# Rotary halves exchanged by ScalarE copies instead of permutation matmuls

## The chip, the cores and the metric

The kernel runs on one core of a Trainium2 chip. The metric is the device time of one execution in microseconds, the median of several runs. The engines are named as in the profile: PE is TensorE (its weight loads are PEld), DVE is VectorE, ACT is ScalarE, POOL is GpSimd, SP is SyncE, whose queue streams the weights. A matmul with fp32 operands is one instruction in the program; the trace shows it as two.

## What is computed

A chain of transformer blocks over 512 tokens of width 1024, all in fp32: a sparse-attention mixer, a state-space mixer, then an "even" mixer, a feed-forward block, an "odd" mixer and a second feed-forward block. The change is in the even mixer, which runs stick-breaking attention (8 heads of 64) and retention (4 heads of 128) on one projection:

```
p = hn @ w_in
sb_q, sb_k, sb_v, r_q, r_k, r_v, r_g = jnp.split(p, cuts, axis=-1)
...
qb = rope(to_heads(r_q, RET_HEADS), pos)
kb = rope(to_heads(r_k, RET_HEADS), pos)
...
def rope(x, pos):
    ...
    x1, x2 = xf[..., :half], xf[..., half:]
    return jnp.concatenate([x1 * cos - x2 * sin, x1 * sin + x2 * cos], axis=-1)
```

With features on the partitions, rope is x * cos + swapped(x) * sin, where swapped(x) has the upper 64 features, negated, in the lower 64 partitions and the lower 64 in the upper.

## The kernel before

Everything is one hand-written program with an instruction list for each engine; nothing schedules them but their order and the semaphores. Activations lie with 128 features on the partitions and the 512 tokens on the free axis. Each product with a weight matrix is done in three fp32r matmuls per 128x128 block: high part of the weights by high part of the input, high by low, low by high. A tile of weights (128 output features, 8 blocks, 512 KB) lands in a ring of four, DVE rounds it to its high part `whi` (L172), POOL subtracts to get `wlo` (L164, L152), and PE multiplies (24 matmuls a tile).

The even mixer has 28 such tiles, seven for each i = 0 to 3: q, k, v of a pair of stick-breaking heads and rq, rk, rv, rg of one retention head. PE runs the first four tiles by themselves (L339 to L341), and the others in quarters of six matmuls (L596 to L598, `product_beside`) between the small matmuls of the attention. `pe_stick` and then `pe_retention` run for each i; a tuple of numbers says how many quarters come between their steps. In `pe_retention` three quarters (18 matmuls) stand between the swap matmuls and the scores; for i = 3, where no tiles are left, three blocks of the next stage's product (9 matmuls, L989 to L991, `pe_even_out_beside`) stand there instead.

The steps around the change, for each i:

- ACT: take rv out of PSUM (L822), then rg with a Silu (L743), which has a table load ahead of it, and a second table load behind it (L794) back to the set with Exp and Ln; then take the stick-breaking output from bank 7 (`eo_h`, L825), once PE has done its last stick matmul (L728, semaphore `e_o`).
- DVE: rqt and rkt by the cosine (L916, into `et`), the rounding of a weight tile, then `eo_l` (L919), the low part of the stick output, which waits for L825 (semaphore `e_oh`); then, in `dve_retention`, the products of the swapped halves with the sine (L1032, from banks 2 and 3 into `el`), and the sums (L1035) that make the rotated query `rqs` and key `rks`; then the scores by the decay (L1039).
- PE: the stick output (L728), the swap matmuls (L950) of rqt and rkt with the 128x128 permutation `swap` into banks 2 and 3, the quarters, the four score matmuls (L955), which wait for both sums of L1035 (semaphore `r_qkv`), more quarters, the weighted sum (L960), and so on to `eo_l` of the retention head (L1054).

At the start of the stage `act_even` issues three loads on ACT's queue, `etab` (tables), `egain` and `swap`, and waits for all three (L759) before it takes the first tile with L736 (Square) and L737 (Copy); L737 frees the accumulator for PE's third tile. PE waits for the same three loads once, at L647.

Of the kernel before, what the change touches and what calls it, by code (L numbers as in the profile page):

```python
# [14 lines left out]
P = 128  # L15
# [32 lines left out]
def build(nc, A, out, names=tuple(s[0] for s in STAGES)):  # L48
# [5 lines left out]
    with ExitStack() as ctx:  # L54
# [32 lines left out]
        def at(name, shape, dt=F32, offset=None):  # L87

            size = int(np.prod(shape[1:])) * 4
            offset = used[0] if offset is None else offset  # L90
            used[0] = offset + (size + 63) // 64 * 64
            assert used[0] <= nc.sbuf_usable_end, (name, used[0])
            return nc.alloc_sbuf_tensor_at(name, shape, dt, offset=offset)
# [416 lines left out]
        decay = etab[:, 3 * P + 2 * S:3 * P + 6 * S].rearrange("p (r s) -> p r s", r=4)  # L510
        e64eps = etab[:, 3 * P + 6 * S:3 * P + 6 * S + 1]
        egain = at("egain", [P, 3])
        swap = at("swap", [P, P])
        eq, ek, ev = (at(name, [P, S]) for name in ("eq", "ek", "ev"))
        rqt, rkt, rvt, rgt = (at(name, [P, S]) for name in ("rqt", "rkt", "rvt", "rgt"))
        qs = at("qs", [P, S])
# [113 lines left out]
        def even_taken(engine, name, i):  # L630

            r = even_tile(name, i)
            engine.wait_ge(acc_free[r % 2], freed(O0["even_in"] + r))
# [10 lines left out]
        def pe_head_squares(pe, i):  # L644

            if i == 0:
                pe.wait_ge(e_loaded, 48)  # L647
            for j in range(2):
                pe.wait_ge(e_sqr, 2 * i + j + 1)
                nc.tensor.matmul(bank[2 + j][:], bdiag, et[:, 2 + j, :], start=True, stop=True).then_inc(e_ms, 1)  # L650
# [104 lines left out]
        def act_even(act):  # L755
            act.dma_start(etab[:], A["even_tables"]).then_inc(e_loaded, 16)
            act.dma_start(egain[:], A["even_gains"]).then_inc(e_loaded, 16)
            act.dma_start(swap[:], A["swap"]).then_inc(e_loaded, 16)
            act.wait_ge(e_loaded, 48)  # L759
            act_head_tile(act, "q", 0, eq)  # L760
            act_head_tile(act, "k", 0, ek)
            act_even_tile(act, "v", 0, sq[:, 0, :])
            act.preload_act_table_set(LOG_EXP)
            act_head_rstd(act, 0)
            act_even_tile(act, "rq", 0, rqt[:])
            for i in range(4):
                act_stick(act, i)
                act_retention(act, i)

        def act_stick(act, i):  # L770

            def soft(u):
                hd, jb, w = unit(u)
                act.wait_ge(e_z, 8 * i + u + 1)
                if u >= 2:
                    act.wait_ge(e_t, 8 * i + u - 1)
                if u == 1 and i:
                    act.wait_ge(r_m, i)
                nc.scalar.activation(ea[:, hd, 0:w], bank[2 + u % 3][:, 0:w], ACT.Abs).then_inc(e_abs, 1)
                act.wait_ge(e_abs, 2 * (8 * i + u) + 1)  # L780
                nc.scalar.activation(ea[:, hd, 0:w], ea[:, hd, 0:w], ACT.Exp, scale=-1.0).then_inc(e_abs, 1)
                act.wait_ge(e_abs, 2 * (8 * i + u) + 2)
                nc.scalar.activation(el[:, hd, 0:w], ea[:, hd, 0:w], ACT.Ln, bias=ones[:, 0:1]).then_inc(e_l, 1)

            def weight(u):
                hd, jb, w = unit(u)
                act.wait_ge(e_t2, 8 * i + u + 1)
                nc.scalar.activation(packed(ew, hd, jb), et[:, u % 4, 0:w], ACT.Exp).then_inc(e_w0, 1)

            def tile(place):  # L790
                name = dict(zip("ACEF" if i else "BDF", EVEN[3:] if i else EVEN[4:])).get(place)
                if name == "rg":
                    act_even_tile(act, "rg", i, rgt[:], ACT.Silu)
                    act.preload_act_table_set(LOG_EXP)  # L794
                elif name is not None:
                    act_even_tile(act, name, i, {"rq": rqt[:], "rk": rkt[:], "rv": sq[:, 1, :]}[name])

            soft(0)
            soft(1)
            tile("A")  # L800
            act.wait_ge(tv_turned, TV0["even_in"] + 2 * i + 1)
            nc.scalar.activation(ev[:], bank[7][:], ACT.Copy).then_inc(tv_taken, 1)
            soft(2)
            soft(3)
            tile("B")
            weight(0)
            weight(1)
            soft(4)
            soft(5)
            tile("C")  # L810
            weight(2)
            weight(3)
            tile("D")
            soft(6)
            soft(7)
            weight(4)
            weight(5)
            tile("E")
            weight(6)
            weight(7)  # L820
            act.wait_ge(tv_turned, TV0["even_in"] + 2 * i + 2)
            nc.scalar.activation(rvt[:], bank[4][:], ACT.Copy).then_inc(tv_taken, 1)  # L822
            tile("F")
            act.wait_ge(e_o, i + 1)
            nc.scalar.activation(eo_h[:, i, :], bank[7][:], ACT.Copy).then_inc(e_oh, 1)  # L825

# [117 lines left out]
        def pe_retention(pe, i, beside):  # L944

            between = iter((3, 4, 2, 3) if i < 3 else (3, 3, 1, 7))
            pe.wait_ge(e_t, 8 * i + 8)
            for j in range(2):
                even_taken(pe, ("rq", "rk")[j], i)
                nc.tensor.matmul(bank[2 + j][:], swap[:], (rqt, rkt)[j][:], start=True, stop=True).then_inc(r_rot, 1)  # L950
            beside(next(between))
            pe.wait_ge(tv_taken, TV0["even_in"] + 2 * i + 2)
            pe.wait_ge(r_qkv, 2 * i + 2)
            for jb in RORDER:
                nc.tensor.matmul(retention_scores(jb), rks[:, jb * P:(jb + 1) * P], rqs[:, jb * P:S],  # L955
                                 start=True, stop=True).then_inc(r_s, 1)
            beside(next(between))
            for jb in range(4):
                pe.wait_ge(r_w, 4 * i + RORDER.index(jb) + 1)
                mm = nc.tensor.matmul(bank[6][:, jb * P:S], rvt[:, jb * P:(jb + 1) * P], packed(ew, 0, jb),  # L960
                                      start=jb == 0, stop=jb == 3)
            mm.then_inc(r_o, 1)
            beside(next(between))
            pe.wait_ge(r_sq, i + 1)
            nc.tensor.matmul(bank[5][:], ones, ea[:, 0, :], start=True, stop=True).then_inc(r_ms, 1)
            if i < 3:
                pe_head_squares(pe, i + 1)
            beside(next(between))
# [59 lines left out]
        def dve_retention(dve, i):  # L1028

            for j in range(2):  # L1030
                dve.wait_ge(r_rot, 2 * i + j + 1)
                nc.vector.tensor_tensor(el[:, j, :], bank[2 + j][:], sin_t, ALU.mult).then_inc(r_part, 1)  # L1032
            for j in range(2):
                dve.wait_ge(r_part, 4 * i + 3 + j)
                nc.vector.tensor_tensor((rqs, rks)[j][:], et[:, j, :], el[:, j, :], ALU.add).then_inc(r_qkv, 1)  # L1035
            dve.wait_ge(e_o, i + 1)
            for jb in RORDER:
                dve.wait_ge(r_s, 4 * i + {0: 1, 2: 2}.get(jb, 4))
                nc.vector.tensor_tensor(packed(ew, 0, jb), retention_scores(jb), decay[:, i, 0:S - jb * P],  # L1039
                                        ALU.mult).then_inc(r_w, 1)  # L1040
            if i < 3:
                dve_even_split(dve, "q", i + 1)
                dve_even_split(dve, "k", i + 1)
            dve.wait_ge(r_r, i + 1)
            nc.vector.scalar_tensor_tensor(et[:, 0, :], bank[6][:], egain[:, 2:3], ea[:, 1, :],
                                           ALU.mult, ALU.mult).then_inc(r_m, 1)
            dve.wait_ge(r_m, i + 1)
            even_taken(dve, "rg", i)
            nc.vector.tensor_tensor(rmix[:], et[:, 0, :], rgt[:], ALU.mult).then_inc(r_mix, 1)
            if i < 3:  # L1050
                dve_head_scaled(dve, i + 1)
                dve_even_split(dve, "v", i + 1)
            dve.wait_ge(r_hi, i + 1)
            nc.vector.tensor_tensor(eo_l[:, 4 + i, :], rmix[:], eo_h[:, 4 + i, :].bitcast(F32),  # L1054
                                    ALU.subtract).then_inc(r_lo, 1)
# [1941 lines left out]
        dec.append(np.where(d >= 0, np.exp(lg * np.maximum(d, 0)) * P ** -0.5, 0.0))  # L2997
    return np.concatenate([bd, later, before, cc, sc, *dec, np.full((P, 4), 64e-6)], 1).astype(np.float32)

def host_swap():  # L3000

    w = np.zeros((P, P), np.float32)
    for m in range(64):
        w[m + 64, m] = -1
        w[m, m + 64] = 1
    return w

def by_state(v):

    n = v.ndim  # L3010
# [8 lines left out]
def host_arrays(I, names):  # L3019
# [8 lines left out]
        cv[:, l, 3] = cols(I['ffn_conv_b_2'][l])  # L3028
    a['conv'] = cv
    a['even_tables'] = host_even_tables()  # L3030
    a['swap'] = host_swap()
    q, k = I['sb_q_gain_2'][0], I['sb_k_gain_2'][0]
    a['even_gains'] = np.stack([np.concatenate([q, q]), np.concatenate([k, k]), I['ret_out_gain_2'][0]], 1)
    p, c = np.arange(P)[:, None], np.arange(S)[None, :] % P
# [46 lines left out]
```

## Time and profile before

| | |
|---|---|
| median of 3 runs | 2058.25 us (2058.07 to 2058.46) |
| the profiled execution | 2057.75 us, its span 2055.9 us |
| PE busy | 1969.3 us (96%) |
| DVE busy | 1113.0 us (54%) |
| POOL busy | 793.9 us (39%) |
| ACT busy | 607.0 us (30%) |

The span goes from the first to the last instruction of the trace; the profiled execution is 1.85 us longer than its span. The even mixer lies between 760 and 1060 us of it. In the timelines a row gives start, duration, engine, line of the kernel, operation, output and input, and in brackets how long the engine was idle before it and who released it. The starts of PE's matmuls are what counts: their ends are modelled, so that a matmul of 0.39 us may be followed by the next after 0.23.

### The profile page before, as it was taken

The numbers are of one execution on the slowest core, as the hardware profiler recorded it, in microseconds if no ns is written. First come the engines' busy times: TensorE is split into PE (matmuls) and PEld (weight loads), VectorE is DVE, ScalarE is ACT, GpSimd is POOL, SyncE is SP. The second block draws the span as 40 slices with busy tenths as digits, with TensorE's granted clock in tenths as the row PEclk, the third lists the DMA queues.
The fourth block names the chain that finished last, engine by engine and source line by source line (L and its number), as shares of the span: only waits on it lengthen the run. The fifth ranks groups of instructions, "written<-read, shape, count | busy, mean of one in ns | idle before, by whom it ended". The sixth has DMA issues, their size and how long they took to land.

```text
span 2055.9 us, 26747 instructions
## 1 busy us (share of the span) xinstructions
PE 1969.3 (96%) x9876; PEld 1531.0 (74%) x9876; DVE 1113.0 (54%) x2063; ACT 607.0 (30%) x1164; POOL 793.9 (39%) x430
## 2 busy tenths in 40 slices
PE   8999999978999969999999999999999999999999
PEld 5867776757778746766678888887578878888887
DVE  5679998886774444445565454312533355454311
ACT  3136656125651135444422111100422222111100
POOL 3532222336663433222234444444133234444443
PEclk9999999989999989999999999999999999999999
DMA  5611111212212222111122232333122122222232
GB/s 182 178 62 42 33 41 42 82 51 66 71 49 95 92 66 83 62 62 51 52 82 94 92 102 92 102 102 104 62 72 69 66 84 93 99 95 95 100 123 72
DMA packets 55300, 167.66 MB, mean 82 GB/s; under 512 B 8080, under 2 KB 16144, under 8 KB 54816
## 3 DMA queue, kind: packets, MB, share of 16 engines
q1 hardware_dynamic: 47904, 155.22, 22.4%
q10 hardware_dynamic: 7296, 11.09, 2.0%
q8 instruction: 65, 1.06, 0.2%
q14 instruction: 35, 0.29, 0.0%
HBM read 157.90 MB, written 2.10 MB: 78 GB/s over the span
## 4 chain that ended last, share of the span: by engine, by line
issue 38%; PE 34%; POOL 15%; DVE 8%; SPq 4%; DMA 0%; POOLq 0%; ACT 0%; DVEq 0%; ACTq 0%
POOL wlo L164 14%; PE bank L181 7%; PE bank L182 7%; PE bank L183 7%; SPq L146 4%; DVE prob L1674 2%; DVE ssb L1661 2%; PE bank L2655 1%; PE bank L2656 1%; PE bank L2657 1%; PE bank L1296 1%; PE bank L1321 1%; PE bank L1239 1%; PE bank L1237 1%; DVE probt L1682 1%
## 5 line engine op out<-in xcount | busy, mean ns | idle before, releaser
L164 POOL TENSOR_TENSOR wlo<-raw,whi 128x1024 fp32r<-128x1024 f32 x248 | 597.7, 2410 | 957.4 <-DVE whi L172 957.4
L172 DVE CAST whi<-raw 128x1024 fp32r<-128x1024 f32 x288 | 203.8, 708 | 418.3 <-PE bank L183 227.6
L181 PE MATMUL bank<-xh,whi 128*128 128x512 f32 x704 | 276.3, 392 | 8.8 <-POOL wlo L164 8.8
L182 PE MATMUL bank<-xl,whi 128*128 128x512 f32 x704 | 275.3, 391 | 0.0
L183 PE MATMUL bank<-xh,wlo 128*128 128x512 f32 x704 | 275.2, 391 | 0.0
L596 PE MATMUL bank<-xh,whi 128*128 128x512 f32 x424 | 177.1, 418 | 1.5 <-POOL wlo L164 1.5
L598 PE MATMUL bank<-xh,wlo 128*128 128x512 f32 x424 | 166.1, 392 | 0.0
L597 PE MATMUL bank<-xl,whi 128*128 128x512 f32 x424 | 165.3, 390 | 0.0
L181 PEld LDWEIGHTS bank<-xh,whi 128*128 128x128 f32 x704 | 133.0, 189 | 38.1 <-POOL wlo L164 10.1
L183 PEld LDWEIGHTS bank<-xh,wlo 128*128 128x128 f32 x704 | 133.1, 189 | 28.1
L182 PEld LDWEIGHTS bank<-xl,whi 128*128 128x128 f32 x704 | 133.2, 189 | 27.3
L183 PE MATMUL bank<-ghi,wlo 128*128 128x512 f32 x352 | 139.1, 395 | 0.0
L181 PE MATMUL bank<-ghi,whi 128*128 128x512 f32 x352 | 139.0, 395 | 0.0
L182 PE MATMUL bank<-glo,whi 128*128 128x512 f32 x352 | 139.0, 395 | 0.0
L1722 POOL TENSOR_TENSOR wlo<-raw,whi 128x1024 fp32r<-128x1024 f32 x22 | 52.0, 2364 | 151.7 <-DVE whi L172 151.7
L596 PEld LDWEIGHTS bank<-xh,whi 128*128 128x128 f32 x424 | 79.7, 188 | 27.5 <-issue 13.2
L598 PEld LDWEIGHTS bank<-xh,wlo 128*128 128x128 f32 x424 | 79.6, 188 | 17.7
L597 PEld LDWEIGHTS bank<-xl,whi 128*128 128x128 f32 x424 | 79.9, 188 | 16.4 <-issue 2.2
L1674 DVE TENSOR_SCALAR prob<-prob,gsig,stat 128x128 f32<-128x128 f32 (+3 forms) x128 | 89.3, 739 | 2.3
L478 DVE TENSOR_TENSOR upad<-bank,rstd 128x512 f32<-128x512 f32 x44 | 30.5, 693 | 102.7 <-PE bank L183 87.4
L225 ACT ACTIVATE bank<-h 128x512 f32<-128x512 f32 x42 | 25.2, 601 | 205.8 <-DVE h L402 199.3
L491 DVE TENSOR_TENSOR bank<-bank,rstd 128x512 f32<-128x512 f32 x44 | 30.8, 699 | 99.4 <-PE bank L183 94.3
(387 smaller groups left out, 3900.7 us busy)
## 6 DMA issues: line engine op xcount, KB each, us to landing
raw<-in_weights_dram SPq DMA_DIRECT2D x288, 512.0 KB, 3.2
h<-in_x_dram SPq DMA_DIRECT2D x2, 1024.0 KB, 7.4
sz<-su SPq DMA_DIRECT2D x128, 16.0 KB, 1.8
out_dram<-h ACTq DMA_DIRECT2D x4, 512.0 KB, 2.6
etab<-in_even_tables_dram ACTq DMA_DIRECT2D x1, 1730.0 KB, 6.5
x_kh<-kvc_h ACTq DMA_DIRECT2D x2, 256.0 KB, 5.0
x_kl<-kvc_l ACTq DMA_DIRECT2D x2, 256.0 KB, 7.0
x_vh<-kvc_h ACTq DMA_DIRECT2D x2, 256.0 KB, 5.0
```

What stands on the lines that cost most here:

```text
L146: sp.dma_start(sz[32 * r:32 * r + 32, j, q * P:(q + 1) * P], su[32 * q:32 * q + 32, j, r * P:(r + 1) * P]).then_inc(s_ub[j % 4], 16)
L164: nc.gpsimd.tensor_tensor(wlo[:, s % 2, :], raw[:, s, :], whi[:, s % 2, :].bitcast(F32), ALU.subtract).then_inc(w_lo, 1)
L172: nc.vector.tensor_copy(whi[:, t_of_4 % 2, :], raw[:, t_of_4, :]).then_inc(w_hi, 1)
L181: nc.tensor.matmul(to, w_h, pe_h, start=first and k == 0, stop=False)
L182: nc.tensor.matmul(to, w_h, pe_l, start=False, stop=False)
L183: last_mm = nc.tensor.matmul(to, w_l, pe_h, start=False, stop=last and k == chunks - 1)
L596: nc.tensor.matmul(to[:], w_h, xh[:, k, :], start=k == 0, stop=False)
L597: nc.tensor.matmul(to[:], w_h, xl[:, k, :], start=False, stop=False)
L598: mm = nc.tensor.matmul(to[:], w_l, xh[:, k, :], start=False, stop=k == KC - 1)
L1661: nc.vector.tensor_tensor_reduce(ssb[:, br, hd, 0:w], bank[2 + c][:, 0:w], dist[:, i % 2, hd, (3 - qb) * P:S], -1.0, 3e38, ALU.add, ALU.mi ...
L1674: mul = nc.vector.tensor_scalar(prob[:, br, hd, 0:w], prob[:, br, hd, 0:w], gsig[:, qb, g:g + 1], stat[:, 8 + 2 * br + hd:9 + 2 * br + hd] ...
L1722: nc.gpsimd.tensor_tensor(wlo[:, r % 2, :], raw[:, r % 4, :], whi[:, r % 2, :].bitcast(F32), ALU.subtract).then_inc(w_lo, 1)
```

## The change

The permutation matrix goes, with its load, its tile and its eight fp32 matmuls. In their place ACT copies, for each of rqt and rkt, the upper 64 partitions with scale -1 into the lower 64 of a PSUM bank, and the lower 64 into the upper 64: four copies of 64x512 for each i, in a new function that stands between the second table load and the copy of the stick output. `r_rot` now counts four a head instead of two.

```diff
@@ pe_head_squares
-                pe.wait_ge(e_loaded, 48)
+                pe.wait_ge(e_loaded, 32)
@@ act_even
-            act.dma_start(swap[:], A["swap"]).then_inc(e_loaded, 16)
-            act.wait_ge(e_loaded, 48)
+            act.wait_ge(e_loaded, 32)
@@ new
+        def act_halves(act, i):
+
+            act.wait_ge(e_t, 8 * i + 8)
+            for j in range(2):
+                even_taken(act, ("rq", "rk")[j], i)
+                for half in range(2):
+                    there, here = slice(64 * half, 64 * half + 64), slice(64 - 64 * half, 128 - 64 * half)
+                    nc.scalar.activation(bank[2 + j][there, :], (rqt, rkt)[j][here, :], ACT.Copy,
+                                         scale=1.0 if half else -1.0).then_inc(r_rot, 1)
@@ act_stick
             tile("F")
+            act_halves(act, i)
             act.wait_ge(e_o, i + 1)
             nc.scalar.activation(eo_h[:, i, :], bank[7][:], ACT.Copy).then_inc(e_oh, 1)
@@ pe_retention
-            pe.wait_ge(e_t, 8 * i + 8)
-            for j in range(2):
-                even_taken(pe, ("rq", "rk")[j], i)
-                nc.tensor.matmul(bank[2 + j][:], swap[:], (rqt, rkt)[j][:], start=True, stop=True).then_inc(r_rot, 1)
             beside(next(between))
@@ dve_retention
-                dve.wait_ge(r_rot, 2 * i + j + 1)
+                dve.wait_ge(r_rot, 4 * i + 2 * j + 2)
```

ACT's instructions for i = 0, from the table load ahead of the Silu on, before:

```order
L743 ACT_TABLE_LOAD
L743 ACTIVATE rgt<-bank 128x512
L794 ACT_TABLE_LOAD
L825 ACTIVATE eo_h<-bank 128x512
L736 ACTIVATE et<-bank 128x512
```

and after (with the line numbers of the changed kernel: L742 is L743 of before, L775 is in `act_halves`, L834 is L825 of before):

```order
L742 ACT_TABLE_LOAD
L742 ACTIVATE rgt<-bank 128x512
L802 ACT_TABLE_LOAD
L775 ACTIVATE bank<-rqt 64x512 x2
L775 ACTIVATE bank<-rkt 64x512 x2
L834 ACTIVATE eo_h<-bank 128x512
L735 ACTIVATE et<-bank 128x512
```

Four copies stand between the second table load and the copy of the stick output `eo_h`.

PE's instructions for i = 0, from the last stick matmuls on, before:

```order
L728 MATMUL bank<-ew,ev 64x256 x2
L728 MATMUL bank<-ew,ev 64x128 x2
L950 MATMUL bank<-rqt,swap 128x512
L950 MATMUL bank<-rkt,swap 128x512
L596 MATMUL bank<-xh,whi 128x512
L597 MATMUL bank<-xl,whi 128x512
L598 MATMUL bank<-xh,wlo 128x512
```

and after:

```order
L727 MATMUL bank<-ew,ev 64x256 x2
L727 MATMUL bank<-ew,ev 64x128 x2
L595 MATMUL bank<-xh,whi 128x512
L596 MATMUL bank<-xl,whi 128x512
L597 MATMUL bank<-xh,wlo 128x512
```

The two swap matmuls are gone, and the quarters follow the stick output directly. DVE's instructions and their order are the same.

ACT's queue at the start of the stage, before:

```order
L756 DMA etab<-in_even_tables_dram 128x3460
L757 DMA egain<-in_even_gains_dram 128x3
L758 DMA swap<-in_swap_dram 128x128
L736 ACTIVATE et<-bank 128x512
L737 ACTIVATE eq<-bank 128x512
L736 ACTIVATE et<-bank 128x512
L737 ACTIVATE ek<-bank 128x512
```

and after:

```order
L755 DMA etab<-in_even_tables_dram 128x3460
L756 DMA egain<-in_even_gains_dram 128x3
L735 ACTIVATE et<-bank 128x512
L736 ACTIVATE eq<-bank 128x512
L735 ACTIVATE et<-bank 128x512
L736 ACTIVATE ek<-bank 128x512
```

One load less stands ahead of the first tile.

## Rows read from the trace of the kernel before

**Rows 1.** The page: busy us, share of the span, instructions of each engine.
```profile
PE 1969.3 (96%) x9876; PEld 1531.0 (74%) x9876; DVE 1113.0 (54%) x2063; ACT 607.0 (30%) x1164; POOL 793.9 (39%) x430
```

**Rows 2.** Timeline of PE, i = 0 and 1: start us, us, line.
```profile
821.68 1.12 PE L950 MATMUL bank<-rqt,swap 128*128 128x512 f32 x2
...
823.73 0.39 PE L597 MATMUL bank<-xl,whi 128*128 128x512 f32 x1
...
827.63 2.32 PE L955 MATMUL bank<-rqs,rks 128*128 128x512 f32 x8
...
885.49 1.12 PE L950 MATMUL bank<-rqt,swap 128*128 128x512 f32 x2
...
891.43 1.02 PE L955 MATMUL bank<-rqs,rks 128*128 128x512 f32 x2
```

**Rows 3.** Timeline of ACT, i = 0.
```profile
820.10 1.28 ACT L794 ACT_TABLE_LOAD   x1
821.80 0.60 ACT L825 ACTIVATE eo_h<-bank 128x512 fp32r<-128x512 f32 x1 [0.42 <-PE bank L728]
```

**Rows 4.** Timeline of DVE, i = 0; one release of PE, i = 1.
```profile
822.43 0.69 DVE L919 TENSOR_TENSOR eo_l<-bank,eo_h 128x512 fp32r<-128x512 f32 x1 [2.25 <-ACT eo_h L825]
...
824.91 0.68 DVE L1035 TENSOR_TENSOR rks<-et,el 128x512 f32<-128x512 f32 x1
...
874.88 0.42 DVE L870 TENSOR_TENSOR esp<-esp 128x256 f32<-128x256 f32 x1
...
875.44 1.10 PE L694 MATMUL bank<-esp,etab 128*128 128x512 f32 x2 [1.86 <-DVE esp L870]
```

**Rows 5.** ACT copies by source line (ns min/median/max), and timeline.
```profile
L1410 ACT ACTIVATE bank<-rstd x1: 597/597/597, 47.9 to 47.9; 128x512 f32<-128x512 f32 x1
...
L2683 ACT ACTIVATE xb<-taps x16: 626/630/635, 472.8 to 573.3; 64x512 f32<-64x512 f32 x16
...
L2724 ACT ACTIVATE sq<-bank x32: 249/268/273, 485.1 to 585.8; 32x128 f32<-32x128 f32 x32
...
512.62 1.15 ACT L2724 ACTIVATE sq<-bank 32x128 f32<-32x128 f32 x4 [3.05 <-PE bank L2578]
513.79 1.28 ACT L2683 ACTIVATE xb<-taps 64x512 f32<-64x512 f32 x2
```

**Rows 6.** Timeline of PE, i = 3.
```profile
1014.78 1.12 PE L950 MATMUL bank<-rqt,swap 128*128 128x512 f32 x2
...
1018.84 2.40 PE L955 MATMUL bank<-rqs,rks 128*128 128x512 f32 x8
```

**Rows 7.** Stage start: timelines of ACT, PE, POOL; DMA to landing, us.
```profile
767.82 0.86 ACTq L757 DMA_DIRECT2D egain<-in_even_gains_dram  x1
...
775.21 0.60 ACT L736 ACTIVATE et<-bank 128x512 f32<-128x512 f32 x1 [7.15 <-DMA swap<-in_swap_dram]
775.70 0.59 ACT L737 ACTIVATE eq<-bank 128x512 f32<-128x512 f32 x1
...
776.44 0.47 PE L339 MATMUL bank<-xh,whi 128*128 128x512 f32 x1 [0.36 <-ACT eq L737]
...
773.50 2.39 POOL L152 TENSOR_TENSOR wlo<-raw,whi 128x1024 fp32r<-128x1024 f32 x1 [4.07 <-DVE whi L172]
...
egain<-in_even_gains_dram ACTq DMA_DIRECT2D x1, 1.5 KB, 6.4
```

**Rows 8.** Windows: busy us of PE, PEld, DVE, ACT, POOL; clock, DMA.
```profile
873.50:880.50 7.00, 5.14 (x20) 3.29 (x20) 5.83 (x15) 3.22 (x6) 2.37 (x1) 1.00 0.00 0
1001.00:1008.00 7.00, 5.14 (x11) 2.35 (x11) 4.45 (x11) 2.16 (x4) 2.35 (x1) 0.76 0.01 4
1482.70:1489.70 7.00, 5.51 (x31) 4.71 (x31) 3.19 (x5) 1.02 (x2) 3.76 (x2) 1.00 0.42 130
1649.70:1656.70 7.00, 5.16 (x16) 4.02 (x16) 5.37 (x4) 2.48 (x4) 4.27 (x2) 0.76 0.33 109
1033.50:1041.50 8.00, 5.47 (x18) 4.31 (x18) 6.10 (x5) 2.49 (x4) 4.74 (x2) 0.79 0.34 117
```

More of the change, by code:

```diff
@@ L512, in build @@
         egain = at("egain", [P, 3])
-        swap = at("swap", [P, P])
         eq, ek, ev = (at(name, [P, S]) for name in ("eq", "ek", "ev"))
@@ L2998, in host_even_tables @@
     return np.concatenate([bd, later, before, cc, sc, *dec, np.full((P, 4), 64e-6)], 1).astype(np.float32)
[L3000 to L3006, printed above, removed]
 def by_state(v):
@@ L3030, in host_arrays @@
     a['even_tables'] = host_even_tables()
-    a['swap'] = host_swap()
     q, k = I['sb_q_gain_2'][0], I['sb_k_gain_2'][0]
```

## The prediction

> **What bounds the kernel now.** I read first the page: of the span of 2055.9 us, in a profiled execution of 2057.75 us, TensorE (PE) is busy 96% and ScalarE (ACT) 30% [rows 1]. PE is the bound almost everywhere, so a microsecond that PE gains or waits is a microsecond of the kernel, unless somebody else releases its next instruction. The change lives in one stage, the even mixer, and there in one place that comes four times, once per head pair i: the retention's rotary step. So I read next the timelines of PE, ACT and VectorE (DVE) there.
>
> Call T the moment at which the first swap matmul starts on PE: 821.68 for i = 0. The second head pair repeats the intervals (885.49 to 891.43 where the first has 821.68 to 827.63) and so does the third; only the fourth, with T at 1014.78, differs. On PE [rows 2] the two swap matmuls begin at T and the product behind them runs at its steady pace again from T+2.05 (823.73), and the first of the score matmuls L955 starts at 827.63 = T+5.95. Nothing is idle there. Beside it, ACT finishes a table load at 820.10 + 1.28 = 821.38 = T-0.30 and stands still until the stick-breaking output is there, when it takes it (L825) at T+0.12 [rows 3]. DVE waits for that copy: L919 at T+0.75, then the two products with the sine (L1032), then the two sums L1035, the second of which ends at 824.91 + 0.68 = 825.59 = T+3.91 [rows 4]. That end releases L955. Today it comes 2.0 us before PE arrives. This slack of 2.0 us, and not PE's load, is what the change spends.
>
> **Part 1: PE loses eight matmuls.** From T to T+2.05, less the 0.23 us that one product matmul takes anyway, is 1.8 us per head [rows 2], 7.3 us in the kernel. That is all that can be gained, and it is gained only if PE's next dependent instruction, L955, is ready 1.8 us earlier: PE would arrive there at T+4.15 (i < 3). In i = 3 there are 9 product matmuls in between instead of 18, L955 starts at 1018.84 = T+4.06 [rows 6], and PE would arrive at T+2.3.
>
> **Part 2: ACT gets four copies per head, ahead of L825.** They need rqt and rkt and free banks, all long there, so they start at once behind the table load, at T-0.27. What does one cost? A full-width Copy from SBUF to PSUM took 597 ns, a 64-partition copy from SBUF to SBUF 630 ns [rows 5]: half the partitions save nothing, and I take 0.60 us. What counts is the distance between starts. Two full-width ACT instructions overlap by about 0.1 us (775.21 and 775.70, 0.49 apart [rows 7]). The pair of 64-partition copies L2683, which go to different halves of the partitions as the new ones do, does not: two of 0.63 fill 1.28 us, 0.65 apart, and four of 32 partitions (L2724, 0.27 us each) fill 1.15 us, 0.29 apart [rows 5]. No row has a copy whose input and output partitions differ. I take the nearest, L2683's behaviour with the PSUM duration: 0.62 per copy, 2.48 for four. The bounds are 0.49 (full width) and 0.65.
>
> The Trainium skill, ScalarE: Activation LUTs, section What ACT_TABLE_LOAD costs, says that ACTIVATEs in a row overlap by about 93 ns and gives 186 ns + 0.833 ns per element. By it a copy would take 0.61 us and four 2.08 us, and the forecast would be some 2 us lower; the full-width rows agree with it, the rows of different partition halves do not.
>
> **Part 3: what is queued behind them.** ACT is in order, so L825 starts at T-0.27+2.48 = T+2.21 instead of T+0.12, 2.09 us late. DVE is in order too and takes L919, which waits for L825, ahead of L1032: so both sine products wait 2.09 us, though the halves of q are there long before. The second L1035 ends at T+6.00, and L955 starts 0.14 us behind, at T+6.14; that is the distance between the end of DVE's L870 at 874.88 + 0.42 and the start of the L694 that it releases, 875.44 [rows 4].
> - i = 0, 1, 2: 6.14 against 5.95, +0.2 us each, +0.6 us. The 1.8 us that PE saves turns into an idle stretch of about the same length in front of L955.
> - i = 3: 6.14 against 4.06, +2.1 us. Here only nine matmuls cover the chain. What follows L955 (scores, output, norm, eo_l, then the rest of even_out on PE) hangs on it in a row, so all of it is late.
>
> **Part 4: the swap load goes.** At the start of the stage ACT waits for three loads; the last to land is swap, and ACT begins L736 at 775.21. PE then waits for L737 and starts its third tile at 776.44, 0.36 us idle [rows 7]. Without swap the last is egain, issued at 767.82 and 6.4 us on its way: 774.2, so L737 ends 1.0 us earlier and is out of the way. Late next is the low part of the weights from GpSimd, 773.50 + 2.39 = 775.89, so PE starts near 776.03: -0.4 us. The DVE waits change only their numbers, and the instruction list of ACT has as many table loads as before: nothing for these.
>
> **Part 5: PE's clock.** New idle time on PE can bring its clock to 1.2 GHz. In this trace stretches with about 1.5 us idle (1482.7) kept 1.00; with 1.84 to 1.86 us one kept it (873.5) and two did not (1001, where 5.14 us of 7 were busy, and 1649.7, each 0.76 over the stretch); with 2.5 us (1033.5) it fell as well [rows 8]. A fall that finds PE busy costs about 0.24 x 7 = 1.7 us. The new idle stretches in i = 0 to 2 are T+4.3 to T+6.1, 1.7 to 1.8 us: on the edge. In i = 3 it is T+2.4 to T+6.1, 3.7 us: I count a fall as certain, and 1.3 us for it, since part of the slow time will lie in the wait.
>
> The Trainium skill, TensorE: Matmul & The Clock Gate, Part 1, says that the clock is gated to half when the array has been idle and is let up again under load. The rows show just that, and it is a rule that speaks against trading PE work for a wait.
>
> **The sum:** -0.4 + 0.6 + 2.1 + 1.3 = +3.6 us. On the profiled 2057.75 us that is 2061.35; on the median 2058.25 (0.5 above the profile) 2061.85. I forecast 2061.6, no measurable change, though on its slow side. About 0.2%, 4.1 us, is what a measurement of this kernel can tell from none.
>
> **Rivals.**
> - *The slow side: idle on the edge.* If one of the 1.7 us stretches in i = 0 to 2 lets the clock fall, each adds 1.7 us: 2063.3 for one, 2065.0 for two. It decides from one fall on. For it: two of three stretches with 1.85 us did so. Against: the one with 1.5 us did not, and 1.7 lies between. Chance 0.22.
> - *Copies overlap like full-width ones.* Four at 0.49 to 0.52 end 0.45 us earlier: i = 0 to 2 become -0.2 each, i = 3 +1.7. Sum -0.4 - 0.6 + 1.7 + 1.3 = +2.0: 2060.0. For it: most ACT pairs. Against: L2683 and L2724. Chance 0.17.
> - *Fewer falls of the clock.* The fall at 1003 depends on where idle time lies, and that is moved by tenths of a microsecond; if it stays away, or the one in i = 3 does, 1.3 to 1.7 us are missing: 2059.9; both, 2058.5. Chance 0.12.
> - *The copies hold nobody.* If rks were ready at T+4.15 in each head, PE would keep all 7.3 us: 2057.75 - 7.3 - 0.4 = 2050.1. That needs L919 not to stand in front of L1032, or L825 not behind the copies; the order of both engines says otherwise. Chance 0.04.
> - The forecast itself: 0.45.
>
> **How the numbers follow.** Slower by over 0.2% (above 2062.4) is the first rival, 0.22, and 0.08 of the forecast's own spread (0.65 a copy instead of 0.62, a full 1.7 for the fall): 0.30. Faster is the fourth, 0.04. The rest, 0.66, is within 0.2%. The range 2058.8 to 2063.6 takes in the second and third rival and one fall of the first; outside lie two falls, both falls missing, and the fourth rival, under 0.2 together.
>
> **What would show it.** The copies 0.62 us apart and L825 at 2.2 us behind the end of the last stick-breaking matmuls show part 2; 0.5 apart, the second rival. A PE wait in front of the scores, released by DVE's second sum, about 1.7 us long in three heads and 3.7 in the fourth, shows part 3; no such wait shows the fourth rival. The granted clock behind each shows part 5. The wait for the loads should end near 774.2, and PE's wait for L737 be gone. Most wrong would be a copy across partition halves that costs far more than 0.6 us: each 0.1 us on a copy is 0.4 us in each head, 1.6 us in all.

## The result and the profile after

Over 20 executions of each kernel the changed one has a median of 2061.31 us and the one before 2057.14 us. The ratio is 1.0019, with a 95% interval of 1.0011 to 1.0028: slower by 3.9 us, between 2.3 and 5.8. Forecast were +3.6 us and "within 0.2%", and the measured ratio stands right at the edge of that band, on its inner side.

Single executions of one kernel differ by several microseconds (standard deviation 2.3 us before, 2.8 us after). The profiled execution of the changed kernel happens to be a short one, 2057.11 us with a span of 2055.3 us, less than the profiled one before. So the two traces may not be compared by their spans, only interval by interval. A likely reason why single executions differ, PE's clock, is seen below.

The place of the change, i = 0, on ACT, DVE and PE (timeline: start us, duration us, engine, line; L742, L802, L834, L928, L1037, L1040 and L960 are the kernel's L743, L794, L825, L919, L1032, L1035 and L955 of before, L775 the new copies):

```profile
820.60 1.28 ACT L802 ACT_TABLE_LOAD   x1
821.89 1.22 ACT L775 ACTIVATE bank<-rqt 64x512 f32<-64x512 f32 x2
823.14 1.22 ACT L775 ACTIVATE bank<-rkt 64x512 f32<-64x512 f32 x2
824.29 0.58 ACT L834 ACTIVATE eo_h<-bank 128x512 fp32r<-128x512 f32 x1
...
824.90 0.69 DVE L928 TENSOR_TENSOR eo_l<-bank,eo_h 128x512 fp32r<-128x512 f32 x1 [4.22 <-ACT eo_h L834]
825.51 1.28 DVE L1037 TENSOR_TENSOR el<-bank,etab 128x512 f32<-128x512 f32 x2
826.70 0.68 DVE L1040 TENSOR_TENSOR rqs<-et,el 128x512 f32<-128x512 f32 x1
827.30 0.69 DVE L1040 TENSOR_TENSOR rks<-et,el 128x512 f32<-128x512 f32 x1
...
819.88 2.37 PE L727 MATMUL bank<-ew,ev 128*64 128x512 f32 x16
822.18 0.50 PE L595 MATMUL bank<-xh,whi 128*128 128x512 f32 x1
...
828.14 2.39 PE L960 MATMUL bank<-rqs,rks 128*128 128x512 f32 x8 [1.58 <-DVE rks L1040]
```

T, PE's first start behind the stick output, is now 822.18. Against [rows 2 to 4]: the copy of the stick output, which was at T+0.12, is at T+2.11; DVE waits 4.22 us for it instead of 2.25, and both sine products, which need only banks 2 and 3, stand behind that wait. The second sum ends at T+5.81 instead of T+3.91. The scores start at T+5.96, where they were at T+5.95. PE has lost its two swap matmuls and stands idle for 1.58 us. The exchange is even to a hundredth.

In i = 3 there are nine product matmuls in front of the scores. T is 1013.83:

```profile
1013.83 0.51 PE L994 MATMUL bank<-eo_h,whi 128*128 128x512 f32 x1
...
1019.79 3.85 PE L960 MATMUL bank<-rqs,rks 128*128 128x512 f32 x8 [3.59 <-DVE rks L1040]
...
1038.69 0.51 PE L994 MATMUL bank<-eo_h,whi 128*128 128x512 f32 x1 [2.51 <-POOL wlo L164]
```

The scores are at T+5.96 again, but were at T+4.06 [rows 6]: 1.9 us late, behind a wait of 3.59 us. They themselves take 3.85 us instead of 2.40, since the clock has fallen. The windows show it, for the same places as [rows 8] (busy us of PE, PEld, DVE, ACT, POOL, then the granted clock; 1.00 is 2.4 GHz):

```profile
1001.80:1008.80 7.00, 5.14 (x20) 3.23 (x20) 5.84 (x15) 3.15 (x6) 2.38 (x1) 1.00 0.00 1
1017.00:1025.00 8.00, 5.21 (x14) 3.55 (x15) 4.51 (x9) 0.00 (x0) 0.00 (x0) 0.79 0.08 32
1036.20:1044.20 8.00, 5.51 (x24) 4.48 (x25) 6.01 (x5) 2.49 (x4) 4.74 (x2) 1.00 0.35 122
1650.70:1657.70 7.00, 5.16 (x23) 4.18 (x23) 5.34 (x3) 2.49 (x4) 4.24 (x2) 1.00 0.35 112
```

New is the second row, 0.79 over 8 us, which is 1.7 us of PE work lost. The other three are stretches whose idle time is as long as in the trace before, 1.8 to 2.5 us, and in which the clock had fallen there to 0.76 or 0.79 [rows 8]; here it did not. That is 5 us less lost in these three places, of which the rest of the trace gives back a part (0.74 us of it ahead of the stage, in unchanged code).

A stretch of this length keeps the clock in one execution and loses it in another. The changed kernel and those of experiment 4 (cover alone) and experiment 5 have the same instructions up to T of i = 3, and each has a wait of 1.80 to 1.87 us for `esp` in every head pair: the clock fell behind none of them in the first trace, behind that of i = 2 in the second and that of i = 3 in the third. Over all 13 traces it fell behind 12 of these 52 waits, and behind 7 of the 13 waits of 2.5 us in front of the third even_out tile. At 1.7 us a fall these five places alone would spread the executions by 1.7 us (standard deviation), an estimate from these shares that takes them as independent. So this is the likely source of a large part of the spread, but it is not shown. That the falls are independent isn't shown either: in the four kernels that keep the swap load, the clock fell behind the wait for `esp` in i = 3 each time and in no other head pair. And the mean granted clock on record for each execution, in three digits, goes down as the time goes up in the three series of the kernel before (correlation -0.50 to -0.65), but not in the 20 executions of the changed kernel (-0.04).

I call the tail the time from T of i = 3 to the start of the third even_out tile, which PE gets from POOL after a wait of 2.5 us: 1038.69 - 1013.83 = 24.86 us here. In the kernel before T was 1014.78 [rows 6], and that tile (L989) started 21.31 us behind it:

```profile
1036.09 0.50 PE L989 MATMUL bank<-eo_h,whi 128*128 128x512 f32 x1 [2.53 <-POOL wlo L164]
```

So the tail is 3.55 us longer: 1.9 for the later scores and 1.65 for what follows them (18.90 us from the scores to that tile instead of 17.25), which is the clock. This one interval is nearly the whole measured difference.

### The profile page after: what moved, and what is told of

It reads as the page before. It is cut to its first block, busy times and chain, and to the rows that moved or that the text cites. A ratio compares the mean times of both kernels' runs of the same rounds, so it can differ in the third digit from the quotient of the medians.

```text
span 2055.3 us, 26730 instructions
## 1 busy us (share of the span) xinstructions
PE 1960.6 (95%) x9860; PEld 1524.7 (74%) x9860; DVE 1113.2 (54%) x2063; ACT 616.3 (30%) x1180; POOL 794.2 (39%) x430
## 4 chain that ended last, share of the span: by engine, by line
issue 38%; PE 34%; POOL 15%; DVE 8%; SPq 4%; DMA 0%; POOLq 0%; ACT 0%; DVEq 0%; ACTq 0%
POOL wlo L164 14%; PE bank L181 7%; PE bank L182 7%; PE bank L183 7%; SPq L146 4%; DVE prob L1679 2%; DVE ssb L1666 2%; PE bank L2660 1%; PE bank L2661 1%; PE bank L2662 1%; PE bank L1301 1%; PE bank L1326 1%; PE bank L1244 1%; PE bank L1242 1%; PE bank L1243 1%
```

## The experiments

Times of an experiment are ratios to the kernel before on the same chip, with 9 to 12 executions of each against 23 to 32; in microseconds such an interval is some 4 us wide. So the ratio decides on large steps only, and the intervals of the trace on the small ones. Where PE runs at full clock these repeat to some 0.03 us from trace to trace (a head pair of the kernel before takes 63.79 to 63.81 us), except the start of the stage, of which more below.

**1. The copies in i = 3 alone, and in i = 0 to 2 alone.** The kernel before gets the new function, called where `i == 3`, or where `i < 3`; the other head pairs keep the swap matmuls. The diff shows `i == 3`, without the function itself.

```diff
+            if i == 3:
+                act_halves(act, i)
@@ pe_retention
-            for j in range(2):
+            for j in range(0 if i == 3 else 2):
@@ dve_retention
-                dve.wait_ge(r_rot, 2 * i + j + 1)
+                dve.wait_ge(r_rot, 2 * i + (2 * j + 2 if i == 3 else j + 1))
```

> The kernel before with the copies in i = 3 alone; the swap load, the wait for it and the swap matmuls of i = 0 to 2 stay. Theory (the last head pair has only 9 product matmuls as cover, so the copies' delay shows there alone, and the clock falls in the wait): scores of i = 3 start 5.96 us behind the last stick matmuls' end instead of 4.06, +1.9 us, and a stretch at half clock behind it, +1.7; together +3.6 us, nearly all of what the change costs. Rival (the cost is spread over the four head pairs): a quarter of the change, +1.0 us.

Measured: ratio 1.0028 (1.0017 to 1.0038), +5.8 us (3.5 to 7.8). The trace has the scores at T+5.95 behind a wait of 3.58 us, a clock of 0.79, and a tail of 1039.30 - 1014.50 = 24.80 us:

```profile
1020.45 4.00 PE L967 MATMUL bank<-rqs,rks 128*128 128x512 f32 x8 [3.58 <-DVE rks L1047]
...
1039.30 0.51 PE L1001 MATMUL bank<-eo_h,whi 128*128 128x512 f32 x1 [2.52 <-POOL wlo L164]
```

```profile
1018.00:1026.00 8.00, 5.55 (x16) 3.66 (x17) 4.17 (x8) 0.00 (x0) 0.00 (x0) 0.79 0.03 13
```

> The kernel before with the copies in i = 0 to 2 alone; i = 3 keeps its two swap matmuls, and the swap load stays. Theory: 0 us against before, within 0.3: each head pair waits 1.58 us in front of the scores and has saved 1.8 us less a start-up of 0.2 us, and the trace shows the scores 5.95 us behind the stick output as before. Rival (new idle time makes the clock fall in some of the executions in i = 0 to 2 as well): +1 to +3 us, with stretches below full clock behind the waits.

Measured: 0.9997 (0.9986 to 1.0008), -0.6 us (-2.9 to 1.6). The trace has the scores at T+5.95 or 5.96 three times, as predicted, each behind a wait of 1.58 us; the three waits together, from the list of who waited for whom:

```profile
PE bank L967 <- DVE rks L1047: 4.7, 3, 1.6
```

Three of the four head pairs cost nothing and gain nothing; the fourth carries the change. The rival of an even spread, +1.0 us, lies outside the first interval. The rival of the clock in i = 0 to 2 is not borne out: an interval that ends at +1.6 us leaves room for at most one fall on average, and this trace has none there. Nor has any other: in the 13 traces the clock stayed at 1.00 behind all 20 waits of 1.38 to 1.61 us in front of the scores.

**2. No exchange at all.** The four copies are left out and the waits for them with them; PE keeps its wait for `e_t` (not shown in the diff).

```diff
-            act_halves(act, i)
@@ dve_retention
-                dve.wait_ge(r_rot, 4 * i + 2 * j + 2)
```

> The changed kernel without the four copies a head pair: the halves are not exchanged at all, the sine products read what lies in banks 2 and 3. This part of the computation is left out. Theory (the copies hold ACT's copy of the stick output, and with it DVE and the scores): scores 4.15 us behind in i = 0 to 2, no wait of PE, and 4.05 in i = 3 as before: 3 x 1.8 = 5.4 us and 0.3 from the start of the stage less than before, -5.7 us. Rival (PE would wait for something else anyway): within 2 us of before.

Measured: 0.9978 (0.9968 to 0.9988), -4.5 us (-6.6 to -2.5). Scores at T+4.21 in i = 0 to 2, with no wait of PE, and at T+3.98 in i = 3, behind a wait of 1.61 us for the second sum. So the 1.8 us that the removed matmuls free are real in i = 0 to 2. In i = 3 they can't be had even without an exchange, since DVE's chain behind the stick output ends only there. The change gives up what is free entirely to the chain through ACT and DVE.

**3. What in the chain holds the scores: the copies or the order around them?** Two kernels move one instruction each. The first puts `eo_l` on DVE behind the rotary sums, so that the sine products need not wait for the stick output's copy:

```diff
@@ dve_stick
-            dve.wait_ge(e_oh, i + 1)
-            nc.vector.tensor_tensor(eo_l[:, i, :], bank[7][:], eo_h[:, i, :].bitcast(F32), ALU.subtract).then_inc(e_ol, 1)
@@ dve_retention, behind the two sums
+            dve.wait_ge(e_oh, i + 1)
+            nc.vector.tensor_tensor(eo_l[:, i, :], bank[7][:], eo_h[:, i, :].bitcast(F32), ALU.subtract).then_inc(e_ol, 1)
```

> The changed kernel with DVE's low part of the stick output (eo_l) moved from ahead of the sine products to behind the two sums. Theory (what delays the scores is that DVE's instruction for eo_l, which waits for ACT's eo_h, stands in front of the sine products): DVE starts the sine products as the halves land, q at about 1.0 us and k at 2.2 us behind the stick output's end, and the scores start at 4.3 us behind; PE waits 0.1 us in i = 0 to 2 and 2.0 us in i = 3. Against before 3 x -1.65, +0.25 and -0.3 from the start of the stage: -5.0 us, faster by 0.24%. Rival (the copies themselves take the time): the scores at 5.5 us or later, +2 us or more.

Measured: 0.9987 (0.9976 to 0.9999), -2.7 us (-4.9 to -0.2). DVE in i = 3 (T = 1009.05) and the scores behind it:

```profile
1010.01 0.69 DVE L1035 TENSOR_TENSOR el<-bank,etab 128x512 f32<-128x512 f32 x1 [2.46 <-ACT bank L775]
1011.25 0.69 DVE L1035 TENSOR_TENSOR el<-bank,etab 128x512 f32<-128x512 f32 x1 [0.55 <-ACT bank L775]
...
1013.06 0.68 DVE L1040 TENSOR_TENSOR eo_l<-bank,eo_h 128x512 fp32r<-128x512 f32 x1
...
1013.29 3.94 PE L958 MATMUL bank<-rqs,rks 128*128 128x512 f32 x8 [1.87 <-DVE rks L1038]
```

The sine products start at T+0.96 and T+2.20, released by the copies, and the scores at T+4.24, 1.7 us earlier than in the changed kernel, with the same four copies in the same place. So the copies alone are not what costs 2 us; it is the in-order wait of DVE for an instruction that none of its rotary work needs. The expectation of -5.0 us lies just outside the interval (by the medians of the executions the difference is -4.4). In part the cause is a term of my own: PE still waits 1.87 us in i = 3, and in this trace the clock fell there (scores of 3.94 us), which I had not counted. By the intervals it is -1.65 us in each of the three head pairs (the third set against the first two of before) and +1.85 in the tail, -3.1 in all. One trace doesn't show how often the clock falls there. No run moves `eo_l` in the kernel before; its PE has no wait in front of the scores that such a move could shorten.

The second puts ACT's copy of the stick output ahead of the four copies:

```diff
-            act_halves(act, i)
             act.wait_ge(e_o, i + 1)
             nc.scalar.activation(eo_h[:, i, :], bank[7][:], ACT.Copy).then_inc(e_oh, 1)
+            act_halves(act, i)
```

> The changed kernel with ACT's copy of the stick output (eo_h) ahead of the four exchange copies. Theory: eo_h at 0.1 us behind the stick output's end as in the kernel before, the copies from 0.7 to 3.2 us, the second sine product at 3.2, the scores at 5.2 us behind; PE waits 0.9 us in i = 0 to 2 and 2.9 in i = 3, so -0.7 us in each against the changed kernel, -2.9 in all and -0 to +1 against before. Rival (order on ACT makes no difference, the sum of the work is the same): the scores at 5.96 us as in the changed kernel, +3.9.

Measured: 1.0010 (1.0001 to 1.0018), +2.1 us (0.2 to 3.7). The scores are at T+5.27 in all four, after waits of 0.90 us (2.90 in i = 3). The interval takes in what the first expectation says and ends just short of the rival's +3.9; the scores' place fits the first alone: order on ACT is worth 0.7 us a head, order on DVE 1.7.

**4. The cover in i = 3.** The seven blocks of each of the first two even_out tiles are dealt out to the four gaps of `pe_retention` by a tuple. With 6 in place of 3, 18 matmuls instead of 9 stand in front of the scores.

```diff
-            between = iter((3, 4, 2, 3) if i < 3 else (3, 3, 1, 7))
+            between = iter((3, 4, 2, 3) if i < 3 else (6, 1, 1, 6))
```

> The changed kernel with the even_out blocks of i = 3 dealt out as 6, 1, 1, 6 instead of 3, 3, 1, 7: 18 product matmuls instead of 9 in front of its scores. Theory (the cost sits in i = 3 because only nine matmuls cover the copies there): the scores stay at 5.96 us behind the stick output's end, PE's wait in front of them falls from 3.59 to 1.6 us and the clock stays up; -1.9 - 1.7 us and at most +0.4 for a wait in front of the last block: -3.2 against the changed kernel, +0.7 against before. Rival (the nine matmuls taken from behind the scores leave a wait of the same length there): +3 to +4 against before.

Measured: 1.0015 (1.0002 to 1.0028), +3.1 us (0.4 to 5.8), which both expectations fit. The trace tells them apart:

```profile
1021.54 2.39 PE L960 MATMUL bank<-rqs,rks 128*128 128x512 f32 x8 [1.50 <-DVE rks L1040]
...
1037.12 0.50 PE L994 MATMUL bank<-eo_h,whi 128*128 128x512 f32 x1 [2.51 <-POOL wlo L164]
```

```profile
1018.00:1026.00 8.00, 6.50 (x25) 4.15 (x24) 4.87 (x9) 0.27 (x1) 0.00 (x0) 1.00 0.15 58
```

The wait is 1.50 us, the clock stays at 1.00, and the tail is 1037.12 - 1015.58 = 21.54 us: 0.2 more than before and 3.3 less than in the changed kernel. That the executions did not become faster in the same measure stays open; one trace doesn't show how often the clock falls in other places.

With both edits:

> The same dealing, 6, 1, 1, 6, with eo_l behind the rotary sums on DVE as well. Theory: the scores at 4.24 us in all four, no wait of PE in front of any (1.87 us in i = 3 with eo_l moved alone), no fall of the clock there: 4 x -1.7 - 0.3 = -7 us against before, 2050 us, 0.34% faster; the fastest of all. Rival (what is saved in front of the scores is waited for behind them): as with eo_l moved alone, -3 to -5 us.

Measured: 0.9974 (0.9964 to 0.9984), -5.4 us (-7.4 to -3.3), the lowest ratio of the kernels that compute everything (its interval overlaps that of `eo_l` moved alone), and below both the kernel before and the changed one. The interval takes in the -7 of the theory and most of the rival's -3 to -5. T is 1009.62:

```profile
1013.91 2.35 PE L958 MATMUL bank<-rqs,rks 128*128 128x512 f32 x8
...
1029.46 0.66 PE L992 MATMUL bank<-eo_h,whi 128*128 128x512 f32 x1 [2.51 <-POOL wlo L164]
```

```profile
1010.00:1018.00 8.00, 8.00 (x33) 5.60 (x32) 4.96 (x9) 2.27 (x4) 0.57 (x1) 1.00 0.21 66
```

PE has no wait in front of the scores, which are at T+4.29, and the tail is 19.84 us, 1.5 us shorter than before. In the window shown PE is busy 8.00 of 8 us; the idle time that is left lies at the end of the tail, in the wait of 2.51 us for POOL. By the intervals the kernel gains 1.6 us in each head pair and 1.5 in the tail, -6.3 us. The prediction of this kernel took 1.7 for each and 0.3 for the start of the stage. That the executions show -5.4 is within the noise. Its trace has two falls behind the wait for `esp`, in i = 0 and i = 3, a place that this edit doesn't touch.

As a control, the same tuple in the kernel before:

> The kernel before with the same dealing, 6, 1, 1, 6, as a control. Theory: before has no wait in front of the scores of i = 3 with nine matmuls, so nine more only push the scores back by 2.0 us and leave fewer behind them: 0 to +0.5 us. Rival (the dealing by itself is better): -1 us or more, and then a part of the gain of the two kernels above is not of the rotary step.

Measured: 0.9999 (0.9988 to 1.0011), -0.2 us (-2.5 to 2.3); scores at T+6.02, no wait, tail 1036.65 - 1015.13 = 21.52 us. The dealing by itself gives nothing measurable; it only pays where the scores would be waited for.

**5. The clock in i = 3 by itself.** 14 extra matmuls into a bank that the scores overwrite fill the wait.

```diff
+            for _ in range(14 if i == 3 else 0):
+                nc.tensor.matmul(bank[4][:], whi[:, 0, 0:P], xh[:, 0, :], start=True, stop=True)
             pe.wait_ge(r_qkv, 2 * i + 2)
```

> The changed kernel with 14 extra matmuls of 128x512 (fp32r, 3.2 us) into the free bank 4 in i = 3, where PE waits 3.59 us for the rotary sums; their result is overwritten by the scores. Theory (the idle stretch lets the clock fall): the scores start as late as in the changed kernel, 5.96 us behind, but at full clock; from there to the stall of even_out 17.2 us as before instead of 18.9; -1.7 us against the changed kernel, +1.9 against before. Rival (the clock of this place costs nothing, since other stretches below full clock come or go in exchange): no difference to the changed kernel, +3.9.

Measured: 1.0016 (1.0004 to 1.0027), +3.3 us (0.8 to 5.6). This does not tell the two apart. The trace does for its own execution (the scores, then the window over them, and third the same window in the changed kernel):

```profile
1019.72 2.42 PE L962 MATMUL bank<-rqs,rks 128*128 128x512 f32 x8 [0.28 <-DVE rks L1042]
```

```profile
1016.00:1024.00 8.00, 7.72 (x32) 5.59 (x32) 4.86 (x9) 0.54 (x2) 0.00 (x0) 1.00 0.18 62
```

```profile
1016.00:1024.00 8.00, 4.41 (x11) 2.73 (x11) 4.53 (x8) 0.52 (x2) 0.00 (x0) 0.79 0.17 61
```

The scores start as late as in the changed kernel, at T+5.87, and take 2.42 instead of 3.85 us; the tail is 1036.98 - 1013.85 = 23.13 us, 1.7 less. So the idle time of 3.59 us, not the late arrival of the operands, took the clock there. What the kernel as a whole gets from it is not settled, as falls elsewhere come and go.

**6. Do the copies overlap?** The same copies in another order, two into the lower partitions, then two into the upper; a single execution. DVE's waits for the copies change their numbers to match (not shown in the diff).

```diff
-            for j in range(2):
-                even_taken(act, ("rq", "rk")[j], i)
-                for half in range(2):
+            for half in range(2):
+                for j in range(2):
```

> The changed kernel with the four copies in another order: both with output in partitions 0 to 63 first, then both with output in 64 to 127, instead of alternating. Theory (ACT instructions that follow each other overlap by 0.1 us, unless they go to another half of the partitions): the first two and the last two start 0.50 us apart, the middle two 0.62. Rival (the partition shift itself prevents the overlap): all 0.62 apart.

Measured, ACT in i = 0:

```profile
819.74 0.59 ACT L776 ACTIVATE bank<-rqt 64x512 f32<-64x512 f32 x1
820.27 0.58 ACT L776 ACTIVATE bank<-rkt 64x512 f32<-64x512 f32 x1
820.88 0.60 ACT L776 ACTIVATE bank<-rqt 64x512 f32<-64x512 f32 x1
821.41 0.58 ACT L776 ACTIVATE bank<-rkt 64x512 f32<-64x512 f32 x1
821.93 0.58 ACT L835 ACTIVATE eo_h<-bank 128x512 fp32r<-128x512 f32 x1
```

0.53, 0.61 and 0.53 us apart; the scores come 0.2 us earlier, at T+5.76. All four copies shift across partitions, and two pairs overlap all the same, by 0.06 us where two full-width instructions overlap by 0.11 [rows 7]. What takes the overlap away is the change of the output's partition half between two instructions, and not the change of the bank: all three pairs here go from one bank to the other, and only the middle one changes the half. The one execution, of 2055.51 us, says nothing on the time.

**7. The wait for the loads.** In the changed kernel the load of egain goes ahead of that of etab; a single execution.

```diff
-            act.dma_start(etab[:], A["even_tables"]).then_inc(e_loaded, 16)
             act.dma_start(egain[:], A["even_gains"]).then_inc(e_loaded, 16)
+            act.dma_start(etab[:], A["even_tables"]).then_inc(e_loaded, 16)
```

> The changed kernel with the load of egain (1.5 KB) issued ahead of that of etab (1730 KB) at the start of the stage. In the changed kernel the wait for the two ends with egain, 7.1 us after its issue at 768.56, 7.5 us after that of etab. Theory (a small load that is issued behind the large one lands with or behind it, so the large one sets the wait and taking swap away gives little): egain lands in about 2 us, the wait now ends with etab, some 7.0 us after the first issue, 0.5 us earlier. Rival (egain is slow by itself): it is again the last, 6.4 to 7 us behind its issue.

Measured: egain lands in 1.6 us, etab now in 7.3 instead of 6.5. The changed kernel first (timeline with the issue and the end of the wait; then us to landing):

```profile
768.56 0.45 ACTq L756 DMA_DIRECT2D egain<-in_even_gains_dram  x1
775.70 0.60 ACT L735 ACTIVATE et<-bank 128x512 f32<-128x512 f32 x1 [6.90 <-DMA egain<-in_even_gains_dram]
```

```profile
egain<-in_even_gains_dram ACTq DMA_DIRECT2D x1, 1.5 KB, 7.1
```

and with egain first:

```profile
767.07 0.35 ACTq L755 DMA_DIRECT2D egain<-in_even_gains_dram  x1
774.82 0.60 ACT L735 ACTIVATE et<-bank 128x512 f32<-128x512 f32 x1 [7.12 <-DMA etab<-in_even_tables_dram]
```

```profile
etab<-in_even_tables_dram ACTq DMA_DIRECT2D x1, 1730.0 KB, 7.3
egain<-in_even_gains_dram ACTq DMA_DIRECT2D x1, 1.5 KB, 1.6
```

The first half of the theory holds, the second doesn't: the wait ends 7.75 us after the first issue, against 7.52 in the changed kernel and 7.78 in the kernel before. The small load lands late only when it is issued behind the large one. Why etab takes longer here is open. It took 6.5 to 6.7 us in the 12 traces in which another load was issued behind it and 7.3 here, where it is the last; egain took 6.4 us in the four traces with swap behind it and 7.0 to 7.4 in the eight in which it was the last. So it may be the place at the end of the queue, and not the small load ahead, that costs 0.6 to 1.0 us. The wait ended 7.65 to 7.86 us behind the first issue in the four traces with the swap load, and 7.36 to 7.86 in the nine without. All have the load of 1730 KB in it, and none leaves that out, so that it bounds the wait is likely and not shown.

## Why the prediction held, point by point

- **Part 1 (PE freed of 1.8 us a head)** was right for i = 0 to 2: with no exchange at all the scores come 1.74 us earlier (T+5.95 to T+4.21). The 7.3 us "in the kernel" can't be had: in i = 3 PE would be there at T+2.3, and DVE, with no exchange to wait for, lets it start at T+3.98, where it was at T+4.06. So the fourth rival, "PE would keep all 7.3 us" with rks ready at T+4.15, doesn't follow from its own numbers either; three heads make 5.4 us.
- **Part 2 (four copies 0.62 us apart)** was right: two fill 1.22 us, at 596 ns each, and the pairs start 1.25 us apart. The rival of full overlap fell, and experiment 6 shows what its rows and L2683's rows [rows 5] have different. The one miss is at the end: L834, which writes all partitions, starts 0.53 us behind the last copy, not 0.62. (Four copies at 0.52 instead of 0.62 would have made the forecast 1.6 us lower, four heads of 0.4, rather than "some 2 us".)
- **Part 3 (what is queued behind)** was right in mechanism and off by 0.18 us in size. The scores came at T+5.96 instead of T+6.14: 0.1 from L834, the rest from sine products that take 1.28 us for two instead of 1.36. So i = 0 to 2 cost nothing instead of 0.6 us, and i = 3 cost 1.9 instead of 2.1. Both halves are confirmed by experiment 1. Of the remedies, moving `eo_l` brings the scores forward in all four head pairs (experiment 3), and more cover takes away the wait of i = 3 and its fall in the trace, though the executions with cover alone don't show the gain (experiment 4).
- **Part 4 (the swap load)** failed in its step "egain, issued at 767.82 and 6.4 us on its way: 774.2". I carried egain's landing over from a trace in which it had a load behind it. Without that it lands 7.1 us after its issue, and PE's wait for L736 (L737 of before) is still there, 0.38 us. From the start of PE's first tile to T of i = 0 it is 59.04 us after (763.14 to 822.18) and 59.28 before (762.40 to 821.68): -0.24 us, not -0.4. Even that is not resolved: in the traces with no fall in it this interval is 59.19 to 59.39 us with the swap load (four traces) and 58.93 to 59.43 without (six).
- **Part 5 (the clock)** was right for i = 3: it fell after the wait of 3.6 us in the changed kernel and in experiments 1 and 7, for 1.6 to 1.7 us each and not the 1.3 I took. My reason for 1.3, that part of the slow time lies in the wait, fails too: in experiment 6 the clock was down before the scores began, and the fall cost more, 2.7 us (19.99 us from the scores to the third even_out tile instead of 17.25). The edge cases of i = 0 to 2, with 1.58 us idle, kept it in every trace here. The rival "fewer falls" took the falls elsewhere for a property of the kernel; they differ from one execution to the next.
- **The sum.** Forecast -0.4 + 0.6 + 2.1 + 1.3 = +3.6. By the intervals it was -0.24 + 0.15 (two head pairs' lengths, 63.87 and 63.88 us against 63.81 and 63.79) + 1.9 + 1.7 = +3.5, and measured were +3.9 (2.3 to 5.8). (The third head pair can't be compared, since the trace before has a fall in it.) Part 3 was 0.65 us too high, parts 4 and 5 together 0.55 too low, so the closeness of the total is luck in part; the place and the mechanism are not. Luck is also in the absolute 2061.6 against a median of 2061.31: it rests on a median of 3 executions of the kernel before, which over 20 is 1.1 us lower.

The forecast of no change beyond 0.2% is what the ratio of 1.0019 says, but its interval reaches well over 1.002. "Slower by over 0.2%", to which I gave 0.30, is nearly as well supported. And "no measurable change" is wrong as a description: with 20 executions of each kernel the interval lies wholly above 1, so a slowdown of 0.1% to 0.3% was measured.

## What to carry to other kernels

Before moving work off the busiest engine, ask what is queued behind it on the engine that takes it, and on the next one: here four cheap copies held nobody by themselves once 18 matmuls covered them (experiment 4, both edits), but pushed one unrelated copy back, and an in-order wait for that copy held the rotary products. The same copies won 5.4 us once that instruction stood behind them and the last head pair had its cover. And look for the place with the least cover: an edit made four times was paid once, where nine matmuls stood instead of eighteen.

## What the runs showed of the hardware

- ACT instructions that follow each other without a wait overlap by 0.06 to 0.1 us (0.53 apart at 0.59; full width 0.49 at 0.60 [rows 7]) if they write the same partitions or one of them writes all, and not at all (0.61 to 0.62 apart at 0.60) if the second goes to the other half. The shift from one partition half to the other costs nothing in the copy's duration: 596 ns for 64x512 from SBUF to PSUM, where a full 128x512 copy took 597 [rows 5].
- Whether PE's clock falls after 1.8 to 2.5 us of idle time is not fixed by the kernel. In the 13 traces it fell behind 12 of 52 waits of 1.80 to 1.91 us and behind 7 of 13 of 2.5 us, in kernels with the same instructions up to there too. It stayed behind all 20 waits of 1.38 to 1.61 us in front of the scores; it fell behind the one of 1.87 us there (experiment 3) and behind all five of 2.90 to 3.59 us (changed kernel, experiments 1, 3, 6, 7). A fall cost 1.6 to 1.7 us in these, and 2.7 in experiment 6. A trace compared by its span alone would have shown the changed kernel 0.6 us faster.
- A 1.5 KB load took 7.1 us behind a 1730 KB load on the same queue, and 1.6 us ahead of it. The load that was issued last landed 0.6 to 1.0 us later than where another stood behind it (egain 7.0 to 7.4 us against 6.4, etab 7.3 against 6.5 to 6.7).
